# A gated conv and cross-attention layer on one core: host-laid columns and contiguous weight chunks, K made as columns, on-chip transposes dropped

## What is computed

```
def mem_kv(mem, norm_mem, w_k, w_v):
    m = rmsnorm(mem, norm_mem)                  # 256 memory rows
    k = jnp.einsum("bmd,dhe->bmhe", m, w_k)     # K and V are also outputs
    v = jnp.einsum("bmd,dhe->bmhe", m, w_v)
    return k, v

xn = rmsnorm(x, norm_mix)
proj = xn @ w_in                                # 1024 x 10240, split into a_b, a_c, a_x, b_val, b_glu, q, gates
ya, new_a = causal_dwconv(buf_a, a_c * a_x, conv_a_w)          # width 3
yb, new_b = causal_dwconv(buf_b, b_val * sigmoid(b_glu), conv_b_w)   # width 31; new_a, new_b are outputs
...                                             # out projections, cross-attention to k and v, gates, w_o, SwiGLU
```

## Time and profile before

| | |
|---|---|
| time, median of 3 runs | 1056.12 us |
| lowest and highest run | 1055.22, 1056.71 us |
| span of the profiled execution | 1053.4 us |
| around the span (median less span) | 2.7 us |
| TensorE busy | 1042.0 us, 99% of the span |
| VectorE, ScalarE, GpSimd busy | 827.9, 496.1, 112.8 us |
| stage K/V, first matmul to first matmul of stage B | 9.54 to 65.91 us |
| DMA in that stage | busy share 0.93, 285 GB/s |

### The profile page before, as it was taken

The page is one execution under the profiler, slowest core; times in us unless marked ns, Lnnn a source line. Parts: engine busy times, 40 slices in busy tenths (PEclk is TensorE's granted clock), DMA queues, the critical chain, the costliest instruction groups (busy, mean ns, idle before and its releaser), DMA issues.

```text
span 1053.4 us, 20301 instructions
## 1 busy us (share of the span) xinstructions
PE 1042.0 (99%) x8631; PEld 1035.4 (98%) x8631; DVE 827.9 (79%) x1375; ACT 496.1 (47%) x573; POOL 112.8 (11%) x90
## 2 busy tenths in 40 slices
PE   9999999999999999999999999999999999999997
PEld 8999999999999999999999999999999999999996
DVE  6797988888989999898988654588788467788754
ACT  6745554544334344554358632353365235365432
POOL 3671000002300001000000000000000000000000
PEclk9999999999999999999999999999999999999999
DMA  8968777789796777787876834311687345477412
GB/s 295 285 190 194 168 205 205 220 219 307 217 264 152 195 194 169 182 189 170 196 195 145 238 131 139 99 61 61 162 183 170 107 124 127 132 185 187 140 41 82
DMA packets 161452, 182.31 MB, mean 173 GB/s; under 512 B 5158, under 2 KB 151934, under 8 KB 157126
## 3 DMA queue, kind: packets, MB, share of 16 engines
q1 hardware_dynamic: 128422, 106.64, 32.4%
q0 software_dynamic: 8064, 52.17, 25.6%
q10 hardware_dynamic: 24880, 22.26, 6.8%
HBM read 122.34 MB, written 7.54 MB: 123 GB/s over the span
## 4 chain that ended last, share of the span: by engine, by line
PE 95%; DVE 3%; ACT 1%; issue 1%; ACTq 0%; DVEq 0%
PE acc L2612 32%; PE acc L2630 16%; PE acc L3045 12%; PE acc L2997 11%; PE acc L2798 6%; PE acc L3004 6%; PE acc L2806 3%; PE acc L2723 2%; PE acc L2584 1%; PE acc L2731 1%; PE acc L2877 1%; PE acc L2853 1%; DVE o_acc L1953 1%; PE acc L2716 0%; DVE ubyb L1683 0%
## 5 line engine op out<-in xcount | busy, mean ns | idle before, releaser
L2612 PE MATMUL acc<-big_h,w_h 128*128 128x260 f32 x1344 | 271.7, 283 | 0.1
L2612 PE MATMUL acc<-big_l,w_h 128*128 128x260 f32 x1344 | 270.0, 282 | 0.0
L2612 PEld LDWEIGHTS acc<-big_h,w_h 128*128 128x128 f32 x1344 | 206.6, 188 | 0.6 <-DVE st L1989 0.3
L2612 PEld LDWEIGHTS acc<-big_l,w_h 128*128 128x128 f32 x1344 | 206.9, 188 | 0.0
L1683 DVE SCALAR_TENSOR_TENSOR ubyb<-ubyb,prm 128x512 f32<-128x512 f32 x240 | 180.2, 751 | 7.0
L2630 PE MATMUL acc<-big_h,w_l 128*128 128x260 f32 x1344 | 168.9, 282 | 0.0
L2630 PEld LDWEIGHTS acc<-big_h,w_l 128*128 128x128 f32 x1344 | 164.6, 188 | 0.0
L870 ACT ACTIVATE w_h<-w_raw 128x1024 fp32r<-128x1024 f32 x100 | 100.2, 1051 | 69.7 <-DMA w_raw<-in_w_in_dram 28.8
L2997 PE MATMUL acc<-x_h,ws_h 128*128 128x260 f32 x504 | 125.7, 282 | 0.0
L2997 PE MATMUL acc<-x_l,ws_h 128*128 128x260 f32 x504 | 125.6, 282 | 0.0
L2997 PEld LDWEIGHTS acc<-x_h,ws_h 128*128 128x128 f32 x504 | 94.8, 188 | 0.2 <-ACT cp L1407 0.2
(11 more groups left out here) (368 smaller groups left out, 1830.3 us busy)
## 6 DMA issues: line engine op xcount, KB each, us to landing
w_l<-w_raw POOLq DMA_DIRECT2D x31, 1024.0 KB, 8.2
w_raw<-in_w_in_dram SPq DMA_DIRECT2D x26, 1024.0 KB, 5.7
ws_l<-w_raw POOLq DMA_DIRECT2D x15, 768.0 KB, 6.3
w_raw<-in_w_in_dram SPq DMA_DIRECT2D x20, 512.0 KB, 5.3
k_st<-in_cache_mem_k_dram ACTq DMA_DIRECT2D x8, 1024.0 KB, 8.8
v_st<-in_cache_mem_v_dram ACTq DMA_DIRECT2D x8, 1024.0 KB, 13.6
w_l<-w_raw POOLq DMA_DIRECT2D x10, 768.0 KB, 7.1
w_raw<-in_w_ff_gate_dram SPq DMA_DIRECT2D x18, 256.0 KB, 3.1
```

The source lines that it names most:

```text
L2612: last = M.matmul(out[:, b, 0:HALF], w_h[:, slot, k, cols], xs[:, k_at + k, b * HALF:(b + 1) * HALF], start=start and k == 0 and xs is x[0 ...
```

## The change

The host now sends x, memory and the conv states a second time or only as columns, the parameters as one tensor of 128 rows, and every weight chunk as one tensor whose row for a partition is contiguous (8 KB a partition; before, 1 KB or 512 byte pieces). Rows of x and memory still come, for the sums of squares.

- K is made as columns (`w_h` and the memory operand change places for chunks 0 to 3), scaled by a factor that lies along the row (`rm_rep`), and stored so; the host turns it back. The conv tails are stored as columns from where they lie.
- No input, parameter, K or tail is turned on the chip. Before the stage TensorE runs 34 products of the identity with itself instead of 16 and 10 more.
- The rest of chunks 0 to 7 is made half by POOL, half by DVE (chunk 0 by DVE alone, as before).
- x is scaled by DVE in SBUF as eight instructions of 128x520, its low part made in two of 128x2080, its high part by ACT in two. The conv-state sums moved behind that, and L1702 (adding x's parts together) is gone. The x columns for the residual come straight from the input; the scratch store is gone.

```diff
-WARM, FILL = 16, (4, 6)
+WARM = 34
@@ SP
+            first_half(0, w_first)
+            first_half(1, w_loaded[0])
             rows(0, mem_prompt[0, 0:P, :])
             rows(1, mem_prompt[0, P:2 * P, :])
-            sp.dma_start(w_raw[:, 0, 0:HK, :], wk[:, 0:HK, 0:CW]).then_inc(w_first, 16)
-            sp.dma_start(w_raw[:, 0, HK:KT, :], wk[:, HK:KT, 0:CW]).then_inc(w_loaded[0], 16)
...
+            load(1)
             x_rows(0)
             x_rows(1)
+            load(2)
             x_rows(2)
+            x_rows(3)
+            rows(6, xs_dram)
+            load(3)
+            x_columns(0)
+            load(4)
+            x_columns(1)
+            load(5)
+            sp.dma_start(sb_x[:, :, :], state_b_t[:, :, :]).then_inc(sb_in, 16)
+            sp.dma_start(sa_x[:, :, :], state_a_t[:, :, :]).then_inc(sa_in, 16)
+            for c in range(6, C_OB):
+                load(c)
@@ POOL
-                    for s in range(2):
+                    for s in range(1 if c < C_B else 2):
@@ ACT
+            act.dma_start(prm_f[:, :], params).then_inc(prm_in, 16)
...
+            act.wait_ge(prm_in, 16)
+            memory_hi(0)
+            first_chunk_hi(0, w_first)
+            memory_hi(1)
+            first_chunk_hi(1, w_loaded[0])
+            squares(0, P)
             squares(1, P)
...
             for c in range(8):
+                if c:
+                    split(c + 1, (c + 1) % 2)
+                    if c in (1, 2):
+                        root(c)
+                    kv_out(c - 1)
                 if c == 1:
                     for n in (4, 5, 6):
                         squares(n, TS if n == 6 else P)
+                if c in (5, 6):
+                    x_high(c - 5)
+            kv_out(7)
@@ DVE
             for c in range(8):
+                if c < 7:
+                    chunk_lo(c + 1, 1)
...
+                if c == 4:
+                    rr = T["rr"]
+                    done(rr)
+                    V.tensor_copy(r_rep[:, 0:2 * P], acc[rr % 4][:, 0, 0:2 * P])
+                    V.tensor_copy(r_rep[:, 2 * P:TOK], acc[rr % 4][:, 1, 0:TOK - 2 * P]).then_inc(acc_read, 1)
+                    dve.wait_ge(acc_read, rr + 1)
+                    x_scaled(0)
+                kv_scaled(c)
                 if c:
-                    prep(c - 1)
+                    kv_low(c - 1)
...
+                if c == 4:
+                    x_scaled(1)
+                if c in (5, 6):
+                    x_low(c - 5)
+            kv_low(7)
@@ PE
+                for h in range(2):
+                    pe.wait_ge(w_hi, 2 * c + h + 1)
+                    for n in range(2):
+                        if c == 0:
+                            pe.wait_ge(mem_lo if n else mem_hi, h + 1)
+                        last = kv_high(c, h, n)
                 last.then_inc(hi_used, 1)
...
+                kv_end(c)
-            pe.wait_ge(nrm_lo, 5)
+            pe.wait_ge(x_lo, 2)
@@ PE, queries of head 0, and behind stage X
-                if h == 0:
-                    use = T["btail"]
-                    free(use)
-                    pe.wait_ge(acc_read, T["b"] + 16)
-                    flip8_back(use, lambda k: ubyb[:, k + 1, :], slice(SLOT - TS - PAD, SLOT), PAD + TS)
...
-            use = T["ctail"]
-            free(use)
-            pe.wait_ge(u_used, 1 + KT)
-            flip8_back(use, lambda k: ua_tail[:, k, :], slice(0, TS + 2), TS + 2)
```

More of the change, by code:

```diff
@@ L731, in _ @@
-            for j in range(4):
-                load(C_GB + j, j % 2, win, COL_GATE + BR_B * D + j * CW)
-            for j in range(4):
-                load(C_OB + j, j % 2, wob, j * CW)
+            x_rows(3)
[7 more added lines that the diff above has]
+            sp.dma_start(sa_x[:, :, :], state_a_t[:, :, :]).then_inc(sa_in, 16)
@@ new lines, in kv_high @@
+            def kv_high(c, h, part_x):
+                out, ks = acc[T[f"kv{c}"] % 4], range(h * HK, (h + 1) * HK)
+                for j in range(2):
+                    cols = slice(j * P, (j + 1) * P)
+                    for k in ks:
+                        if c < 4:
+                            last = M.matmul(out[:, j, 0:N_MEM], w_h[:, c % 2, k, cols], mn[part_x][:, k, :],
+                                            start=k == 0 and part_x == 0, stop=False)
+                        else:
+                            last = M.matmul(out[:, j, 0:CW], mn[part_x][:, k, cols], w_h[:, c % 2, k, :],
+                                            start=k == 0 and part_x == 0, stop=False)
+                return last
@@ new lines, in kv_end @@
+            def kv_end(c):
+                out = acc[T[f"kv{c}"] % 4]
+                for j in range(2):
+                    cols = slice(j * P, (j + 1) * P)
+                    for k in range(KT):
+                        if j == 0 and k == 0 and c:
+                            pe.wait_ge(w_sub, subtracted(c))
+                        if j == 0 and (k == HK or c == 0 and k == 0):
+                            pe.wait_ge(kv_sub, kv_subtracted(c) if k else 1)
+                        if c < 4:
+                            last = M.matmul(out[:, j, 0:N_MEM], w_l[:, c % 2, k, cols], mn[0][:, k, :],
+                                            start=False, stop=k == KT - 1)
+                        else:
+                            last = M.matmul(out[:, j, 0:CW], mn[0][:, k, cols], w_l[:, c % 2, k, :],
+                                            start=False, stop=k == KT - 1)
@@ L2718, in _ @@
-                for m in range(2 if c else 0):
-                    rows = slice(m * P, (m + 1) * P)
-                    for n, k in itertools.product(range(2), range(KT)):
-                        if m == 0 and n == 0 and k % HK == 0:
-                            pe.wait_ge(w_hi, 2 * c + k // HK + 1)
-                        last = M.matmul(acc[use % 4][:, m, 0:CW], mn[n][:, k, rows], w_h[:, c % 2, k, :],
-                                        start=k == 0 and n == 0, stop=False)
-                last.then_inc(hi_used, 1)
```

650 lines of the change are left out of this document (239 added, 411 removed).

## The result

The changed kernel takes 1058.24 us (median of 13 runs, 1056.86 to 1060.71), the kernel before 1056.12 beside it (13 runs). The ratio is 1.0022, 95% interval 1.0014 to 1.0029: slower by two parts in a thousand, 0.6 us above the forecast of 1057.6. The profiled execution has a span of 1055.9 us, 2.5 more than before, 2.3 us under the median; it took 1057.65 us itself, 1.75 more than its span.

What follows compares the result with a forecast made beforehand. TensorE, busy 99% of the span, was taken to bound the kernel. 1053.4 + 0.9 (stage B) - 0.8 (ctail) + 1.4 (clock) = 1054.9 us of span, with 2.7 around it 1057.6 us; range 1047 to 1061.

Steps and rivals of the forecast that it cites:

- First matmul 7.2: Start of stage K/V: after parameters, half the memory columns and ACT's instructions, first matmul at 7.2 us instead of 9.54.
- A wait of 1.3 us before chunk 1: Stage K/V: TensorE waits 1.3 us for chunk 1's load, landed at 13.8, and goes on at 14.8.
- DMA at 399 GB/s, chunk 5 landed at 36.4: Stage K/V loads: 13.4 MB pass at 399 GB/s up to chunk 5, which lands at 36.4 us.
- Rival B: Stage K/V: loads run at 350 GB/s, chunk 5 lands at 41, stage B near 70; 1061.4 us, chance 0.15.
- DVE's own work 19.0 and POOL's blocks 8.0: Before stage B, from 39.8: DVE's work to the second x_low takes 19.0 us, POOL's port-holding subtractions add 8.0.
- Stage B at 66.8: Stage B waits for the second x_low and starts at 66.8 us, 0.9 later than before; bounds 64.0 to 69.0.
- Clock 1.4: After TensorE's new 6.4 us gap before stage B, a lowered granted clock costs 1.4 us; bounds 0 and 2.0.
- btail 0: Before the first score product: removing btail's eight products gains 0, as that product waits for DVE's q_l; bounds 0 and 0.8.
- ctail -0.8: Behind stage X: ctail's eight products, bare between two chunks at 0.79 us, go, for -0.8 us.
- Behind stage B's start nothing: After stage B's start: no effect expected; x combinations and state sums come early enough, and TensorE waits for no load.
- The 2.7 us that the sum puts around the span: Outside the span: 2.7 us added to the 1054.9 us of span to give 1057.6 us.
- Rival A: Before stage B: DVE's instructions fit between, wait under 1 us, no clock lost, stage B at 57.5; 1046.9 us, chance 0.25.

Runs made afterwards that it cites:

- e6: The changed kernel with the parameters' load issued first on SP's queue instead of on ACT's; 1060.47 us.
- e4: The changed kernel with K/V chunks 2 to 7 moved by DMA in pieces of 1 KB, not 8 KB; 1060.46 us.
- e3: The changed kernel with 27 identity products on TensorE in its wait before stage B; 1057.25 us.
- e9: The changed kernel with the plain chunks 8 to 59, behind K/V, moved in pieces of 1 KB, not 8 KB; 1056.09 us.
- e10: e8 with POOL's halves of the subtractions of chunks 5, 6 and 7 made by DVE as well; 1049.93 us.
- e11: e10 with both x_low behind chunk 7's subtraction and the low part of chunk 5's V behind them; 1048.61 us.
- e7: The changed kernel with chunks 8 and 9's low parts by DMA, first x scalings ahead of chunk 5's subtraction, second behind chunk 6's; 1052.98 us.
- e8: e7 with chunk 8's low part made by DVE behind the second x_low and only chunk 9's by DMA; 1051.19 us.

## Why the prediction was right

The forecast, slightly slower with nearly all of the gain turned into one wait before stage B, held. The measured 2.1 us is clear of noise (interval 1.5 to 3.1), and the forecast gave "slower" 0.34 and "same" 0.36 (its own terms, 0.15 and a third of 0.60, make 0.35), so the sign was hardly called. Two of its signs of being right missed, the first matmul at 7 to 8 and a wait of 1 to 2 us before chunk 1; the others came. Its steps:

- **First matmul 7.2 (bounds 7.0 to 10.0): 8.43.** The step that was mis-sized first. The parameters landed at 5.7, not below the 4.9 of the memory half, and four ACT instructions took 1.7 us, not 1.1. In e6 a later start was not made up before stage B.
- **A wait of 1.3 us before chunk 1, going on at 14.8:** a wait of 0.6 us, going on at 16.0; its load was there at 14.9, forecast 13.8. The mechanism held, all of it 1.1 us late.
- **DMA at 399 GB/s, chunk 5 landed at 36.4:** 392 to 414 GB/s, landed at 38.5. 1.1 us of it is the start: from 2 to 6 us the DMAs moved 300 GB/s and not 399. The rest is bytes: by 37.8 us 14.1 MB had passed (373 GB/s on average), and the sum had 13.4. SP issues the conv states, 1 MB, at 31.56 right behind chunk 5's load, and the sum left them out; that they are the difference was not tested. Rival B asked for 350 GB/s and falls; e4 shows it in small: at 353 in one stretch the time is 1060.46.
- **DVE's own work 19.0 and POOL's blocks 8.0, together 27.0:** from POOL's end at 42.10 to 67.36 it is 25.3. The four instructions that stood (2.11, 2.08, 2.81 and 4.46, alone 0.68 and 2.31) give blocks of 7.1, which leaves 18.2. I had put one block on the x scalings and the last before the second x_low, two of them in part beside a K/V scaling from PSUM; in this profile they fell on three kv_low and the second x_low. In the six other profiles with the same order up to chunk 6 the first does fall on the x scalings. The number of meetings was right, the places only in part.
- **Stage B at 66.8 (64.0 to 69.0): 67.41.** DVE's sequence started 2.3 us later than forecast and was 1.7 us shorter. The two nearly cancel: that the number came out within 0.6 us is partly luck, the mechanism is not. The waits inside chunks 6 and 7 were forecast at 3.7; there was one, 2.75, and the one in front 5.1, not 6.4.
- **Clock 1.4 (0 to 2.0): 1.5**, isolated by e3.
- **btail 0:** TensorE waits for DVE's qrep 1.18 instead of 0.30 us, which is the 0.8 us of the eight products. **ctail -0.8:** the products are gone, and everything behind the first score product is 0.5 us shorter, not 0.8; where the other 0.3 went is open.
- **Behind stage B's start nothing:** no new wait of TensorE up to the score products. The DMA's contiguous chunks bring nothing there (e9).

Sum measured: +1.5 +1.5 -0.5 = +2.5 us of span, forecast +1.5. The 2.7 us that the sum puts around the span are not that: every run of either kernel that has both numbers lies 1.67 to 1.85 us above its own span, and the other 0.9 is that the profiled execution before was faster than the median. As a step from one median to the other it did no harm. Rival A wanted stage B at 57.5 and 1046.9 us. What kept it away was for the most part that DVE and POOL exclude each other, not TensorE and not DVE's amount of work: with POOL out of the way (e10, e11), DVE's order changed and chunks 8 and 9 made otherwise, stage B starts at 60.0 and 59.6 and the times are 1049.9 and 1048.6, near A's number. What is left, 1.9 us of wait for x_low, is DVE's own work and the loads.

## What to carry to other kernels

Taking work off the bounding engine is worth only what the next one in line can follow: here 9 us of transposes bought a wait for an engine that was busy 78% of the span, but without a gap in the last 27 us of that stage. Before moving an operand from PSUM to SBUF on VectorE, look at what GpSimd runs at that time: for instructions that exclude each other, two engines are not two engines, and giving the whole of a split job to one of them can be faster than sharing it. Where such meetings decide, a microsecond in a load's arrival can decide whether they happen (e9), so read the pairs in the timeline and not the mean of a line.

## What was not expected of the hardware

- The clock fell after short waits in one execution and not in another. In e7, with waits of 1.75 and 1.83 us at 58.3 and 61.9, it was at 0.50 from 60 to 64; in e8, with 1.77 and 1.93 at nearly the same places, at 1.00. In the changed kernel one wait of 2.75 us was followed by a mean of 0.56 over 2.6 us. In e7 the fall came as the second wait began (a mean of 0.89 from 59 to 60 us, 0.50 from 60 on), and in e5 and e10 the clock was at 1.00 behind waits of 2.09 and 1.93 us in front of stage B; what decides between them these runs do not show.
- 172 KB moved ahead of the first loads delayed the first weights' half to 9.03 us and the first matmul by 1.7 us (e6). At the 377 GB/s of that stretch the bytes alone are worth some 0.5 us.
- Slower loads gave a faster kernel (e9), and one kernel's runs fell into two groups of times, 1054.4 to 1055.7 and 1059.3 to 1062.1 us (e4).
- One core alone drew 392 to 414 GB/s for nearly 30 us. The Trainium skill, "HBM Reference", says that a core streaming alone measures well above its share of about 358 GB/s; the trace agrees, and the limit that the prediction weighed does not bind here.
